# The low half of every strip of weights moved 128 bytes along its slot

## The chip, the core and the metric

One core of a Trainium2 chip runs the whole program. The metric is the device time of one execution in microseconds (us).

## What is computed

Three layers over 256 tokens of width 1024, batch 1, all in float32: a retention layer (four heads), a layer of latent attention (16 heads, causal), each with a gated side input, and a block with a 31-tap convolution, a multi-window pooling branch, an output mix and a gated feed-forward network of hidden width 2816. Nearly all of the time goes into products of an activation matrix with a weight matrix:

```python
for i in range(DEPTH):
    h = rms_norm(x, pre_norm_g[i])
    y = retention_branch(h, ...) if i % 2 == 0 else mla_branch(h, ...)
    x = x + rms_norm(y, post_norm_g[i])
    x = x + (p[i] @ ple_w_proj[i]) * jax.nn.sigmoid(x @ ple_w_gate[i])
# second block
proj = h @ w_in;  ...  mix = merged @ w_out
up = causal_dwconv(h @ w_up, w_dw_f, b_dw_f)
v, gt = jnp.split(up, 2, axis=-1)
f = (jax.nn.gelu(gt) * v) @ w_down
```

## The kernel before

The kernel reaches float32 accuracy with the faster float32r products: each operand is split into a high part (rounded to float32r) and a low part (the rest), and each product is made of three: high by high, high by low, low by high.

The weights are cut into 264 blocks of 128 partitions by 1024 elements (768 for the query blocks of the attention layer). SyncE loads a block from HBM into one of four slots of `raw`. ScalarE copies it, rounded, into the slot of the same number in `whi` (L990, in `split`); VectorE subtracts this from `raw` and writes the rest into `wlo` (L1521). TensorE takes the block from there. Both engines split three blocks ahead of TensorE (`AHEAD = 3`). A slot of `whi` or `wlo` is 1024 + 64 elements long (`SLOT_PAD`), so 4352 bytes, which is 17 times 256; the two tensors follow `raw` (4 slots of 4096 bytes) in the memory of each partition.

There are two kinds of block. In a **strip** the weights are the stationary operand: `products` (L486 to L502) takes eight tiles of 128 by 128, and for each issues three matmuls with 256 moving columns, one for each token: `whi` against the high part of the activations (L498), `whi` against their low part (L499), `wlo` against their high part (L500). Each matmul carries a weight load of its own (128 columns), which runs beside the matmul in front of it. In a **row block** the weights are the moving operand, 512 columns at a time, against a stationary tile of activations (`row_products`, L563 to L568, and two loops written out at L703 to L705 and L792 to L794). `row_block(b)` says which kind block b is.

Where a block lies in its slot hangs on the kind. `parts_of(b)` (L300), which both splits call, gives offset 0 for a row block and `STRIP_AT` = 16 elements, 64 bytes, for a strip, the same in `whi` and `wlo`; `products` reads with the same offset. Tiles, activations and slots all begin at multiples of 256 bytes counted from the start of `raw`, so the place of an operand within 256 bytes is 0 for all activations and all row blocks, and 64 for the strips. There is one exception: the first five blocks of the last product (`w_down`, blocks 242 to 246) are used as row blocks, but are split by the code of the loop in front of it, and so count as strips in `row_block`: they are moving operands that begin at 64.

The order of the work is fixed by semaphores (`lo_done` lets TensorE start a block, `pe_done` frees a slot for ScalarE). Some blocks are used unsplit from `raw` as plain float32 and are not touched by the change.

Of the kernel before, what the change touches and what calls it, by code (L numbers as in the profile page):

```python
# [28 lines left out]
P = 128  # L29
# [1 line left out]
D = 1024  # L31
DT = D // P
RING = 4
SLOT_PAD, STRIP_AT = 64, 16
AHEAD = 3
RET_HEADS, RET_V = 4, 512
MLA_HEADS, MLA_NOPE, MLA_ROPE = 16, 128, 64
# [50 lines left out]
def row_block(b):  # L88

    if b < B_RO:  # L90
        return b % 12 in range(4, 8)
    if B_GRP <= b < B_MO:
        return (b - B_GRP) % 12 == 1
    return b < B_MIN + 8 or B_MO <= b < B_WA or B_WO <= b < B_UP or b >= B_DN + 5
# [40 lines left out]
def program(nc, x_in, pre_in, p_in, pos_in, cols_in, rows_in, mask_in, tri_in, cnt_in, ident_in, ada_in, c_row, g_rows, w, out):  # L135

    ctx = ExitStack()
    with ctx:
        def sb(name, shape, dt=F32):
            return ctx.enter_context(nc.sbuf_tensor(name, shape, dt))  # L140
# [6 lines left out]
        whi = sb("whi", [P, RING, 1024 + SLOT_PAD], F32R)  # L147
        wlo = sb("wlo", [P, RING, 1024 + SLOT_PAD], F32R)
# [151 lines left out]
        def parts_of(b, n=1024):  # L300

            if b in KEPT:
                k = KEPT.index(b)
                a = Y[:, 4 * k:4 * k + 4, :, :].rearrange("p k c t -> p (k c t)")
                return a[:, 0:n], a[:, 1024:1024 + n]
            o = 0 if row_block(b) else STRIP_AT
            return whi[:, b % RING, o:o + n], wlo[:, b % RING, o:o + n]

        def used_first(b):

# [175 lines left out]
        def _(pe):  # L486
            mm = nc.tensor.matmul

            def products(base, parts, per=0, i=0, before=(), done=1):


                s = base % RING
                pe.wait_ge(lo_done, base + RING + 1 + per * i)
                for n, (t, a, o, start, stop) in enumerate(parts):
                    if n < len(before) and before[n]:
                        pe.wait_ge(*before[n])
                    c = slice(STRIP_AT + t * P, STRIP_AT + t * P + P)
                    mm(o, whi[:, s, c], a[:, 0, :], start=start, stop=False)  # L498
                    mm(o, whi[:, s, c], a[:, 1, :], start=False, stop=False)  # L499
                    last = mm(o, wlo[:, s, c], a[:, 0, :], start=False, stop=stop)  # L500
                if done:
                    last.then_inc(pe_done, 1)  # L502

# [33 lines left out]
            def strip(base, o, a, per=0, i=0, before=()):  # L537

                products(base, [(k, a[:, k, :, :], o, k == 0, k == 7) for k in range(8)], per, i, before)

            def free_a(k, per=0, i=0):

                pe.wait_ge(act_free, k + 1 + per * i)
                return GA[k % 2]

            def free_d(k, per=0, i=0):

                pe.wait_ge(dve_free, k + 1 + per * i)
                return GD[k % 2]
# [11 lines left out]
            def row_products(base, o, t, a, k0, start, stop, ks=(0, 1)):  # L561

                hi, lo = parts_of(base)  # L563
                for k in ks:
                    c = slice(512 * k, 512 * k + 512)
                    mm(o, a[:, k0 + k, 0, tok(t)], hi[:, c], start=start and k == 0, stop=False)  # L566
                    mm(o, a[:, k0 + k, 0, tok(t)], lo[:, c], start=False, stop=False)  # L567
                    last = mm(o, a[:, k0 + k, 1, tok(t)], hi[:, c], start=False, stop=stop and k == 1)  # L568
                return last
# [110 lines left out]
            b = free_d(V_HEAD + 1)  # L680
# [90 lines left out]
            def group(o, i, gates):  # L771
# [7 lines left out]
                for h in range(4):  # L779
                    out_k = GA[h // 2][:, T * (h % 2):T * (h % 2) + T]  # L780
                    parts += [(2 * h + k, S[:, 2 + k, :, :], out_k, k == 0, k == 1) for k in range(2)]
                pe.wait_ge(act_free, at(A_GRP + 1, 6))
                products(base, parts, 12, i, [None] * 4 + [(act_free, at(A_GRP + 2, 6))])

                pe.wait_ge(mo_gated, at(1, 4))
# [11 lines left out]
                def latent_strip(j, b):  # L797
                    products(base + j, [(k, Y[:, 16 + k, :, :], b, k == 0, k == 5) for k in range(6)],
                             12, i)
# [114 lines left out]
            for j in range(3, 8):  # L914
                if j % 2 == 0:
                    b = free_d(V_WA + j // 2)
                else:
                    b = GD[j // 2 % 2]
                strip(B_WA + j, halves(b)[j % 2], H, before=h_waits(U_LNA) if j == 3 else ())
            for j in range(4):  # L920
                if j % 2 == 0:
                    b = free_a(A_WP + j // 2)
# [4 lines left out]
            with pe.Fori(0, 2) as i:  # L927
                for j in range(4):
                    if j % 2 == 0:
                        b = free_a(A_WG + j // 2, 2, i)  # L930
                    plain_tokens(B_WG + j, halves(b)[j % 2], 4, i)
            for j in range(8, 16):
                if j % 2 == 0:
                    b = free_a(A_WG + j // 2)
# [9 lines left out]
            for j in range(4):  # L944
# [4 lines left out]
                b = bank[j]  # L949
# [25 lines left out]
        def _(act):  # L975
            activation = nc.scalar.activation

            def split(base, n=1024, per=0, i=0):

                b = base + AHEAD  # L980
                if b >= B_END:
                    return
                s = b % RING
                if b in SPARE:
                    act.wait_ge(spare_loaded[SPARE[b]], spare_count(b))
                else:
                    act.wait_ge(raw_loaded[s], raw_count(b) + 16 * (per // RING) * i)
                if b not in KEPT:
                    act.wait_ge(pe_done, used_first(b) + per * i)
                activation(parts_of(b + (per * i if isinstance(i, int) else 0), n)[0], block_in(b, n), ACT.Copy).then_inc(hi_done, 1)  # L990
# [518 lines left out]
        def _(dve):  # L1509
# [4 lines left out]
            def split(base, n=1024, per=0, i=0):  # L1514

                b = base + AHEAD
                if b >= B_END:
                    return
                hi, lo = parts_of(b + (per * i if isinstance(i, int) else 0), n)
                dve.wait_ge(hi_done, b + 1 + per * i)  # L1520
                tt(lo, block_in(b, n), f32(hi), ALU.subtract).then_inc(lo_done, 1)  # L1521
# [948 lines left out]
```

## Time and profile before

| | us |
|---|---|
| median of 3 runs | 828.81 (828.03 to 829.47) |
| the profiled execution, its own time | 828.66 |
| its span, first to last instruction | 826.9 |
| TensorE busy | 811.2 (98%) |
| VectorE busy | 661.9 (80%) |
| ScalarE busy | 456.8 (55%) |

The page counts a matmul as busy from its start to its modelled end, which lies beyond the start of the next one; busy time near 100% says that TensorE always had work, not how fast it took it. The rate shows in the distance from one start to the next. PE is TensorE's matmul stream, PEld its stream of weight loads, DVE VectorE, ACT ScalarE.

### The profile page before, as it was taken

How to read it: one execution, taken by the hardware profiler on the slowest of the kernel's cores; microseconds unless marked ns; L12 is line 12 of the kernel's file. 1: busy time of each engine (PE TensorE's matmuls, PEld its weight loads, DVE VectorE, ACT ScalarE, POOL GpSimd, SP SyncE). 2: the span in 40 equal slices, each digit the busy share in tenths (PEclk: the TensorE clock that was granted, in tenths of full speed). 3: DMA queues.
4: the chain of work that ended last, by engine and by line, in shares of the span. 5: the costliest groups of instructions: out<-in, count | busy, mean ns of one | idle time of the engine just before them, and what ended most of it. 6: DMA issues, size and time to landing. Idle time of an engine off the chain costs nothing.

```text
span 826.9 us, 14985 instructions
## 1 busy us (share of the span) xinstructions
PE 811.2 (98%) x5394; PEld 738.3 (89%) x5394; DVE 661.9 (80%) x1043; ACT 456.8 (55%) x682; POOL 43.4 (5%) x58
## 2 busy tenths in 40 slices
PE   9999999999999999999999999999999999999995
PEld 9898999988778999999988789988988999999884
DVE  5979887786966887787868778999898888888566
ACT  6464545565646665657565636115744777776440
POOL 0009000000011000000000000060000000000000
PEclk9999999999999999999999999999999999999998
DMA  6957675679735747383749572446571665565641
GB/s 223 363 201 265 209 260 190 238 253 361 256 139 166 261 147 268 119 285 111 271 170 335 183 254 106 136 150 212 187 248 58 229 202 182 192 209 207 201 154 51
DMA packets 49002, 170.57 MB, mean 206 GB/s; under 512 B 6080, under 2 KB 6720, under 8 KB 48960
## 3 DMA queue, kind: packets, MB, share of 16 engines
q1 hardware_dynamic: 40896, 143.23, 50.5%
q10 hardware_dynamic: 8064, 26.78, 9.3%
q8 instruction: 26, 0.43, 0.2%
q14 instruction: 16, 0.13, 0.1%
HBM read 168.93 MB, written 1.06 MB: 206 GB/s over the span
## 4 chain that ended last, share of the span: by engine, by line
PE 77%; DVE 13%; ACT 4%; issue 4%; DMA 1%; DVEq 1%; ACTq 0%
PE bank L498 12%; PE bank L500 12%; PE bank L499 12%; PE bank L566 8%; PE bank L568 8%; PE bank L567 8%; DVE bank L2011 4%; DVE wlo L1521 3%; PE bank L512 2%; PE bank L703 2%; PE bank L704 2%; PE bank L705 2%; DVE ada_raw L1533 1%; PE bank L609 1%; PE bank L852 1%
## 5 line engine op out<-in xcount | busy, mean ns | idle before, releaser
L990 ACT ACTIVATE whi<-raw 128x1024 fp32r<-128x1024 f32 (+1 forms) x236 | 244.2, 1041 | 198.3 <-PE bank L500 85.3
L1521 DVE TENSOR_TENSOR wlo<-raw,whi 128x1024 fp32r<-128x1024 f32 (+1 forms) x236 | 282.9, 1211 | 66.3 <-ACT whi L990 64.2
L498 PE MATMUL bank<-H,whi 128*128 128x256 f32 x816 | 230.8, 283 | 0.6 <-DVE wlo L1521 0.4
L499 PE MATMUL bank<-H,whi 128*128 128x256 f32 x816 | 227.7, 279 | 0.0
L500 PE MATMUL bank<-H,wlo 128*128 128x256 f32 x816 | 227.7, 279 | 0.0
L498 PEld LDWEIGHTS bank<-H,whi 128*128 128x128 f32 x816 | 153.8, 189 | 2.1 <-issue 1.2
L499 PEld LDWEIGHTS bank<-H,whi 128*128 128x128 f32 x816 | 154.7, 190 | 0.1
L500 PEld LDWEIGHTS bank<-H,wlo 128*128 128x128 f32 x816 | 153.2, 188 | 0.0
L566 PE MATMUL bank<-whi,Y 128*128 128x512 f32 x216 | 84.9, 393 | 0.3 <-DVE wlo L1521 0.3
L568 PE MATMUL bank<-whi,Y 128*128 128x512 f32 x216 | 84.3, 390 | 0.0
L567 PE MATMUL bank<-wlo,Y 128*128 128x512 f32 x216 | 84.2, 390 | 0.0
L1533 DVE CUSTOM_DVE_ANT_0 ada_raw<-ada_raw,crow 128x1024 f32<-128x1024 f32 x48 | 60.5, 1260 | 6.7 <-DMA ada_raw<-ada_in 6.3
L498 PE MATMUL bank<-Y,whi 128*128 128x256 f32 x176 | 50.1, 284 | 0.4 <-ACT G L1148 0.4
L499 PE MATMUL bank<-Y,whi 128*128 128x256 f32 x176 | 49.2, 280 | 0.0
L500 PE MATMUL bank<-Y,wlo 128*128 128x256 f32 x176 | 49.2, 279 | 0.0
L566 PEld LDWEIGHTS bank<-whi,Y 128*128 128x128 f32 x216 | 40.6, 188 | 9.0 <-DVE wlo L1521 0.7
L568 PEld LDWEIGHTS bank<-whi,Y 128*128 128x128 f32 x216 | 40.6, 188 | 8.7
L567 PEld LDWEIGHTS bank<-wlo,Y 128*128 128x128 f32 x216 | 40.6, 188 | 8.4
L2011 DVE SCALAR_TENSOR_TENSOR bank<-WK,cols,bank 128x256 f32<-128x256 f32 x116 | 47.4, 483 | 0.4
L566 PE MATMUL bank<-whi,H 128*128 128x512 f32 x112 | 44.3, 395 | 0.4 <-DVE H L1592 0.3
L567 PE MATMUL bank<-wlo,H 128*128 128x512 f32 x112 | 43.6, 390 | 0.0
L568 PE MATMUL bank<-whi,H 128*128 128x512 f32 x112 | 43.6, 389 | 0.0
(265 smaller groups left out, 1315.2 us busy)
## 6 DMA issues: line engine op xcount, KB each, us to landing
ada_raw<-ada_in ACTq DMA_DIRECT2D x48, 512.0 KB, 5.2
raw<-w_head SPq DMA_DIRECT2D x47, 512.0 KB, 4.5
raw<-w_up SPq DMA_DIRECT2D x42, 512.0 KB, 3.5
raw<-w_down SPq DMA_DIRECT2D x22, 512.0 KB, 3.4
raw<-w_uq SPq DMA_DIRECT2D x24, 384.0 KB, 3.1
raw<-w_ret_out SPq DMA_DIRECT2D x16, 512.0 KB, 5.1
raw<-w_mla_gate SPq DMA_DIRECT2D x16, 512.0 KB, 4.6
raw<-w_mla_out SPq DMA_DIRECT2D x16, 512.0 KB, 5.3
```

The source lines that it names most:

```text
L498: mm(o, whi[:, s, c], a[:, 0, :], start=start, stop=False)
L499: mm(o, whi[:, s, c], a[:, 1, :], start=False, stop=False)
L500: last = mm(o, wlo[:, s, c], a[:, 0, :], start=False, stop=stop)
L512: last = mm(o[:, tok(t)], raw[:, s, c], WT[:, t, c], start=(k == 0), stop=(k == 7))
L566: mm(o, a[:, k0 + k, 0, tok(t)], hi[:, c], start=start and k == 0, stop=False)
L567: mm(o, a[:, k0 + k, 0, tok(t)], lo[:, c], start=False, stop=False)
L568: last = mm(o, a[:, k0 + k, 1, tok(t)], hi[:, c], start=False, stop=stop and k == 1)
L703: mm(o, Hh[:, kk, tt], whi[:, s, c], start=(kk == 0), stop=False)
L990: activation(parts_of(b + (per * i if isinstance(i, int) else 0), n)[0], block_in(b, n), ACT.Copy).then_inc(hi_done, 1)
L1521: tt(lo, block_in(b, n), f32(hi), ALU.subtract).then_inc(lo_done, 1)
L1533: nc.vector.tensor_tensor_reduce(ada_raw[:, n, :], ada_raw[:, n, :], crow[:], 1.0, 0.0, ALU.mult, ALU.add, macc[:, a:a + 1]).then_inc(ada_ ...
L2011: stt(total[:, c, :], x, w_tap, CT[:, c, :], ALU.mult, ALU.add).then_inc(conv_tap[c], 1)
```

## The change

The one offset for strips becomes two: the high part stays at element 16 (64 bytes), the low part goes to element 48 (192 bytes). Row blocks stay at 0 in both. The slots keep their length: 48 + 1024 elements fit into 1088. No instruction is added, removed or put in another place; the offsets of what VectorE writes at L1521 and of what TensorE reads at L500 change, and, for blocks 242 to 246, of what it reads as the low moving operand at L567.

```diff
-SLOT_PAD, STRIP_AT = 64, 16
+SLOT_PAD, ROW_AT, STRIP_HI, STRIP_LO = 64, 0, 16, 48
...
-            o = 0 if row_block(b) else STRIP_AT
-            return whi[:, b % RING, o:o + n], wlo[:, b % RING, o:o + n]
+            h, l = (ROW_AT, ROW_AT) if row_block(b) else (STRIP_HI, STRIP_LO)
+            return whi[:, b % RING, h:h + n], wlo[:, b % RING, l:l + n]
...
-                    c = slice(STRIP_AT + t * P, STRIP_AT + t * P + P)
-                    mm(o, whi[:, s, c], a[:, 0, :], start=start, stop=False)
-                    mm(o, whi[:, s, c], a[:, 1, :], start=False, stop=False)
-                    last = mm(o, wlo[:, s, c], a[:, 0, :], start=False, stop=stop)
+                    hi = whi[:, s, STRIP_HI + t * P:STRIP_HI + t * P + P]
+                    lo = wlo[:, s, STRIP_LO + t * P:STRIP_LO + t * P + P]
+                    mm(o, hi, a[:, 0, :], start=start, stop=False)
+                    mm(o, hi, a[:, 1, :], start=False, stop=False)
+                    last = mm(o, lo, a[:, 0, :], start=False, stop=stop)
```

## Rows read from the trace of the kernel before

**Rows 1.** The page: busy time by engine, then the chain that ended last.

```profile
PE 811.2 (98%) x5394; PEld 738.3 (89%) x5394; DVE 661.9 (80%) x1043; ACT 456.8 (55%) x682; POOL 43.4 (5%) x58
PE 77%; DVE 13%; ACT 4%; issue 4%; DMA 1%; DVEq 1%; ACTq 0%
```

**Rows 2.** Groups by line, shapes apart, whole span: count, busy us, mean ns, idle before.

```profile
L498 PE MATMUL bank<-H,whi 128*128 128x256 f32 x816 | 230.8, 283 | 0.6 <-DVE wlo L1521 0.4
L498 PE MATMUL bank<-Y,whi 128*128 128x256 f32 x176 | 50.1, 284 | 0.4 <-ACT G L1148 0.4
L498 PE MATMUL bank<-S,whi 128*128 128x256 f32 x40 | 11.5, 287 | 0.7 <-ACT G L1287 0.7
```

**Rows 3.** Timeline of PE, strips of `w_conv_in` and `w_pool_in`: start, length, instruction.

```profile
509.52 0.28 PE L500 MATMUL bank<-H,wlo 128*128 128x256 f32 x1
...
528.22 0.28 PE L500 MATMUL bank<-H,wlo 128*128 128x256 f32 x1
```

**Rows 4.** Timeline of PE, the forty strips of `w_up` (third and last matmul).

```profile
645.18 0.28 PE L500 MATMUL bank<-H,wlo 128*128 128x256 f32 x1
...
757.89 0.28 PE L500 MATMUL bank<-H,wlo 128*128 128x256 f32 x1
```

**Rows 5.** Timeline of PE, slow trains: head gates, attention latents, `w_pool` with `w_pw`.

```profile
50.63 0.28 PE L499 MATMUL bank<-H,whi 128*128 128x256 f32 x1
...
61.70 0.28 PE L500 MATMUL bank<-H,wlo 128*128 128x256 f32 x1
...
278.69 0.28 PE L498 MATMUL bank<-Y,whi 128*128 128x256 f32 x1
...
289.17 0.28 PE L500 MATMUL bank<-Y,wlo 128*128 128x256 f32 x1
...
579.45 0.28 PE L499 MATMUL bank<-H,whi 128*128 128x256 f32 x1
...
590.52 0.28 PE L500 MATMUL bank<-S,wlo 128*128 128x256 f32 x1
```

**Rows 6.** Timeline of PE, `w_down`: blocks 242 to 246, then aligned row blocks.

```profile
758.25 0.40 PE L567 MATMUL bank<-wlo,Y 128*128 128x512 f32 x1
...
772.01 0.40 PE L566 MATMUL bank<-whi,Y 128*128 128x512 f32 x1
...
775.22 0.39 PE L568 MATMUL bank<-whi,Y 128*128 128x512 f32 x1
...
814.89 0.39 PE L566 MATMUL bank<-whi,Y 128*128 128x512 f32 x1
```

**Rows 7.** Groups by line, PEld, 510 to 528 us.

```profile
L498 PEld LDWEIGHTS bank<-H,whi 128*128 128x128 f32 x54 | 10.1, 188 | 0.0
L499 PEld LDWEIGHTS bank<-H,whi 128*128 128x128 f32 x53 | 9.9, 188 | 0.0
L500 PEld LDWEIGHTS bank<-H,wlo 128*128 128x128 f32 x53 | 9.9, 188 | 0.0
```

**Rows 8.** The same, 660 to 740 us.

```profile
L499 PEld LDWEIGHTS bank<-H,whi 128*128 128x128 f32 x227 | 43.6, 192 | 0.0
L498 PEld LDWEIGHTS bank<-H,whi 128*128 128x128 f32 x227 | 42.6, 188 | 0.0
L500 PEld LDWEIGHTS bank<-H,wlo 128*128 128x128 f32 x227 | 42.6, 188 | 0.0
```

**Rows 9.** The splits by line: DVE 660 to 740 and 775 to 815 us, ACT in the latter.

```profile
L1521 DVE TENSOR_TENSOR wlo<-raw,whi 128x1024 fp32r<-128x1024 f32 x30 | 36.6, 1220 | 8.8 <-ACT whi L990 8.8
...
L1521 DVE TENSOR_TENSOR wlo<-raw,whi 128x1024 fp32r<-128x1024 f32 x13 | 15.9, 1226 | 15.4 <-ACT whi L990 15.3
...
L990 ACT ACTIVATE whi<-raw 128x1024 fp32r<-128x1024 f32 x13 | 13.8, 1060 | 20.1 <-PE bank L568 19.9
```

**Rows 10.** Windows: us, then PE, PEld, DVE, ACT, POOL busy (count), granted clock, DMA share, GB/s.

```profile
510.00:528.00 18.00, 18.00 (x162) 18.00 (x160) 17.61 (x35) 5.42 (x9) 0.00 (x0) 1.00 0.55 195
660.00:740.00 80.00, 80.00 (x682) 80.00 (x681) 66.85 (x104) 57.75 (x86) 0.00 (x0) 1.00 0.59 193
759.00:771.00 12.00, 12.00 (x53) 9.74 (x52) 8.21 (x11) 7.07 (x10) 0.00 (x0) 1.00 0.59 189
```

## The prediction

> **What bounds the kernel now.** First the page. TensorE is busy 811.2 of 826.9 us, and the chain that ended last runs through it for 77% [rows 1]. So the time is the number of matmuls times the distance from one start to the next. Then the groups by line: L498 ran 816 + 176 + 40 = 1032 times, and L499 and L500 as often, so strips hold 3096 matmuls of 256 columns; their idle time in front is under 1 us a group [rows 2]. The change touches the operand of 1032 of them.
>
> Then the timeline, for the distance, and here is what the busy shares hide. In the strips of `w_conv_in` and `w_pool_in` 165 steps take 528.22 - 509.52 = 18.70 us, 113.3 ns each [rows 3]. In the strips of `w_up` 957 steps take 757.89 - 645.18 = 112.71 us, 117.8 ns each [rows 4]. It is the same code, slots, tiles of H and offsets, and the granted clock is 1.00 in both [rows 10]. A strip train thus runs in one of two steady rhythms, 4.44 ns apart. The slow one holds in `w_up` (958 matmuls), in three trains like 50.63 to 61.70 us (94 steps in 11.07 us, 117.8 ns), four like 278.69 to 289.17 (89 or 90 steps, 117.8 ns) and one from 579.45 to 590.52 (94 steps) [rows 4, 5]: 958 + 3 x 95 + 4 x 91 + 95 = 1702 matmuls. The other 1394 run at or near 113.3.
>
> The weight loads show what differs. In the fast rhythm the three loads of a triple last 188 ns each [rows 7]; in the slow one the load of L499 lasts 192 and the other two 188 [rows 8], although L498 and L499 load the same tile from the same bytes. So the slow rhythm repeats every three matmuls: 3 x 117.8 = 353.3 ns against 3 x 113.3 = 340.0, which is 13.3 ns more, two steps of 6.67.
>
> That 6.67 ns stands by itself in the last product. Blocks 242 to 246 are moving operands that begin at byte 64 against stationary tiles at 0: 59 steps take 772.01 - 758.25 = 13.76 us, 233.2 ns each. Behind them the moving operand begins at 0 and 175 steps take 39.67 us, 226.7 ns each [rows 6]. A matmul whose two operands stand 64 bytes apart the wrong way costs 6.6 ns more, with all else equal. From this I read that the stream of the moving operand and the load of the next stationary one get in each other's way when both reach the same part of a repeating range of bytes. The range is at most 256 bytes: slots are 17 x 256 bytes apart, and no slot runs differently from the others within `w_up`.
>
> **The change part by part.** *The split on VectorE.* L1521 takes 1220 ns where it writes at 64 and 1226 where it writes at 0 [rows 9]. The output offset is worth 6 ns at most; at 192 I take nothing. Bounds: -6 to +6 ns by the 140 blocks split as strips, under 1 us of VectorE work, and hidden. In `w_up`, where the cover is thinnest, one strip takes 24 x 117.8 = 2.83 us; VectorE is busy 66.85 us in 80, so 2.36 us per strip, ScalarE 57.75, so 2.04 [rows 10]. If TensorE goes to its fast rhythm, a strip takes 24 x 113.3 = 2.72 us and both still fit, so the gain isn't handed to another engine. The DMA moves 193 GB/s there and would need 201. ScalarE's L990 writes where it wrote.
>
> *Blocks 242 to 246.* They hold 60 matmuls, 20 of them with the low part moving. If these 20 lose their 6.6 ns, -0.13 us; if all 60 do, -0.4; if each of the 20 pays it twice, +0.13. I take nothing.
>
> *The low weight load of a strip.* This is the change. No trace of before shows a strip with its low tile at 192, so bounds from the nearest rows. On the good side every slow train goes to the fast rhythm: 1702 x 4.44 ns = 7.6 us less. On the bad side the low load sits 64 bytes on the other side of the moving operand within 256 bytes, the relation of blocks 242 to 246, and each costs 6.67 ns: in the 1394 fast matmuls 465 x 6.67 = 3.1 us more; in all, 1032 x 6.67 = 6.9 us more. If instead the fast trains fall into the slow rhythm, 1394 x 4.44 = 6.2 us more.
>
> Which is likelier? The slow rhythm is one in which three identical loads fall into unequal places, the next triple repeating them. It lives on each load being like the one before. With one load in three displaced by 128 bytes the pattern can't stay as it is in 1702 matmuls, and it is the larger stock: 7.6 us can be won against 6.2 lost. Whether it resolves to 340 ns or to 346.7 (one step of 6.67 left) can't be read off; the latter gives 1702 / 3 x 6.67 = 3.8 us less. I take 3.8, which is also half of the way.
>
> The Trainium skill speaks against any effect. "TensorE: Matmul & The Clock Gate", Part 2, step by step, states that the array has two independent read ports into SBUF, and that loading the next weights takes no bandwidth from the running matmul. "SBUF — State Buffer", Specifications (TRN2), gives 16-byte cachelines, and 64 and 192 are both multiples of 16. By these the sum would be 0. The trace disagrees for a moving operand: 64 bytes cost 6.6 ns [rows 6]. For a stationary one no row decides.
>
> *The sum.* 828.66 (the profiled execution: span 826.9 and 1.8 around it) - 3.8 = 824.9. The median of the runs is 0.15 higher, so 825.0.
>
> **The rivals.**
>
> *Same.* The range that repeats is 128 bytes, not 256. Then 64 and 192 are the same place and nothing changes: 828.8. For it: nothing in the trace tells 128 from 256; slots and tiles begin at multiples of both. Also here: gains and losses cancel, say half of the slow trains won (-3.8) and 3.1 us lost in the fast ones, -0.7. By the skill's rule of separate ports the time would be this one too; the rows bear that rule out for nothing here except the equal length of the splits. Against it: the two rhythms are only 4% apart and start from small differences, so to leave 3096 matmuls untouched asks for exact equality. 0.27.
>
> *Slower.* One mechanism: the low load, now 64 bytes behind the moving operand in place of 64 ahead, meets it, and the matmul beside it waits 6.67 ns. For it: blocks 242 to 246 are that relation and pay it in each of 59 steps [rows 6]. Against it: there the moving operand is 512 columns long and the load takes under half of it. It decides from the point at which more matmuls pay than are freed: 465 in the fast trains alone give +3.1 us, 831.9; if the slow trains keep theirs and all low loads pay, 828.8 + 6.9 = 835.7. The nearer value is 831.9, since in the slow trains two steps per triple are paid already. 0.28.
>
> *The change doesn't do what it says*: not here. Both splits go through `parts_of`, and `products` reads with the same constants.
>
> **How the numbers follow.** Forecast (faster): 0.45 at 825.0, from 821.2 (all slow trains fast) to 827. Same: 0.27. Slower: 0.28, at 831.9. The range must reach from the full gain to most of the slower case: 828.8 - 7.6 - 0.4 = 820.8, and 832.5 above, which leaves out some 0.03 below and 0.12 above (fast trains fallen to the slow rhythm: 835.0; or all low loads paying). The forecast's own range is 821 to 827. A measurement here tells about 0.2%, 1.7 us, from no change. Of the faster case some 0.03 lies within that, and of the slower as much: faster 0.43, same 0.32, slower 0.25.
>
> **What the changed kernel's profile would show.** The distance of starts in `w_up`: 113.3 if the slow rhythm is gone, 115.6 if one step is left, 117.8 if nothing changed, over 118 if the low load pays on top. The distance in the strips of `w_conv_in`: 113.3 if the fast rhythm is untouched, 115.6 if the low load pays, 117.8 if it fell. The weight loads of L498, L499 and L500: if L500 alone now lasts longer, the displaced load is the one that waits. Blocks 242 to 246: whether L567 has a distance of its own. L1521 should stay at 1220 ns, and the idle time in front of L498 under 1 us; if it grows, the cover by VectorE was too thin. The prediction is wrong if the strips' rhythms stand as they were, or if the fast trains are the ones that changed.

## The result: 822.34 us, and every train of strips in the fast rhythm

| | before | changed |
|---|---|---|
| median | 828.26 (824.41 to 829.47, 9 runs) | 822.34 (821.67 to 823.03, 9 runs) |
| ratio, 95% interval | | 0.993 (0.9916 to 0.9944) |
| profiled execution, its span | 828.66, 826.9 | 821.67, 819.6 |

The changed kernel is 0.7% faster. The page, engines first and then the chain, answers to [rows 1]; the instructions are the same in number:

```profile
PE 803.2 (98%) x5394; PEld 729.8 (89%) x5394; DVE 660.8 (81%) x1043; ACT 457.1 (56%) x682; POOL 43.4 (5%) x58
```

```profile
PE 74%; DVE 15%; ACT 4%; issue 4%; DMA 2%; DVEq 1%; ACTq 0%
```

8 us went from TensorE's busy time, and 7.3 us from the span. The timeline of PE of the changed kernel (start, length, instruction; lines are one higher than before) answers to [rows 3], [rows 4], [rows 5] for the first head and [rows 6] for blocks 242 to 246, in that order:

```profile
506.36 0.28 PE L501 MATMUL bank<-H,wlo 128*128 128x256 f32 x1
...
525.08 0.28 PE L501 MATMUL bank<-H,wlo 128*128 128x256 f32 x1
...
642.14 0.28 PE L501 MATMUL bank<-H,wlo 128*128 128x256 f32 x1
...
750.81 0.28 PE L501 MATMUL bank<-H,wlo 128*128 128x256 f32 x1
...
49.59 0.28 PE L500 MATMUL bank<-H,whi 128*128 128x256 f32 x1
...
60.25 0.28 PE L501 MATMUL bank<-H,wlo 128*128 128x256 f32 x1
...
751.15 0.40 PE L568 MATMUL bank<-wlo,Y 128*128 128x512 f32 x1
...
764.74 0.39 PE L567 MATMUL bank<-whi,Y 128*128 128x512 f32 x1
```

The strips of `w_conv_in` and `w_pool_in`, fast before, take 18.72 us for 165 steps: as they were. Those of `w_up` take 108.67 us for 957 steps, 113.6 ns each, where they took 112.71. The head's train takes 10.66 for 94 steps where it took 11.07. Blocks 242 to 246 take 13.59 us for 59 steps, 230.3 ns each, where they took 13.76. (A train is a run of strip matmuls without a wait between them; a step is the distance from one start to the next.)

The fast rhythm isn't there from the first matmul. By the starts in the trace, 22 of the 27 trains of over 30 matmuls begin with some distances of 116 to 124 ns, a dozen at most, and then settle at 113.3; `w_up` has six such distances. Summed over these trains, what lies above 113.33 ns a step is 0.7 us, where before it was 7.7. The weight loads of the changed kernel, 660 to 740 us, answer to [rows 8]:

```profile
L501 PEld LDWEIGHTS bank<-H,wlo 128*128 128x128 f32 x236 | 44.3, 188 | 0.0
L499 PEld LDWEIGHTS bank<-H,whi 128*128 128x128 f32 x236 | 44.3, 188 | 0.0
L500 PEld LDWEIGHTS bank<-H,whi 128*128 128x128 f32 x235 | 44.1, 188 | 0.0
```

None in this window lasts 192 any more, and 236 triples fit where there were 227. The split and the window that holds it answer to [rows 9, 10]:

```profile
L1522 DVE TENSOR_TENSOR wlo<-raw,whi 128x1024 fp32r<-128x1024 f32 x31 | 37.9, 1222 | 6.4 <-ACT whi L991 6.4
```

The window of 660 to 740 us (span, then busy time and count of PE, PEld, DVE, ACT and POOL, clock, DMA share, GB/s):

```profile
660.00:740.00 80.00, 80.00 (x708) 80.00 (x707) 69.19 (x106) 61.01 (x90) 0.00 (x0) 1.00 0.60 208
```

VectorE's split costs what it did (1222 ns against 1220), and its share rose to 86%, but it hands nothing on to TensorE.

One new wait did appear. In the timeline of the changed kernel, at the fifth strip of `w_up`, ScalarE's row in a fence of its own and the rows of PE behind it:

```profile
652.07 0.60 ACT L1477 ACTIVATE WK<-bank 128x512 f32<-128x512 f32 x1
```

```profile
652.70 0.28 PE L501 MATMUL bank<-H,wlo 128*128 128x256 f32 x1
652.91 0.36 PE L499 MATMUL bank<-H,whi 128*128 128x256 f32 x1
653.10 0.28 PE L500 MATMUL bank<-H,whi 128*128 128x256 f32 x1
653.22 0.28 PE L501 MATMUL bank<-H,wlo 128*128 128x256 f32 x1
```

The fifth strip writes the bank of the first again and has to wait until ScalarE has copied it out (L1477, which ends at 652.67). The profile doesn't name this wait, but seven of the fourteen traces of this study have a pause at this matmul, of 200 to 406 ns from start to start, and in each the next matmul starts 0.24 or 0.29 us after the end of that copy. TensorE arrives there 0.4 us earlier than in the slow rhythm and loses 0.2 us with the restart behind it.

### The profile page after: what moved, and what is told of

It is laid out like the page before. It is cut to its first block, busy times and chain, and to the rows that moved or that the text cites. A ratio compares the mean times of both kernels' runs of the same rounds, so it can differ in the third digit from the quotient of the medians.

```text
span 819.6 us, 14985 instructions
## 1 busy us (share of the span) xinstructions
PE 803.2 (98%) x5394; PEld 729.8 (89%) x5394; DVE 660.8 (81%) x1043; ACT 457.1 (56%) x682; POOL 43.4 (5%) x58
## 4 chain that ended last, share of the span: by engine, by line
PE 74%; DVE 15%; ACT 4%; issue 4%; DMA 2%; DVEq 1%; ACTq 0%
PE bank L499 11%; PE bank L501 11%; PE bank L500 11%; PE bank L567 9%; PE bank L569 8%; PE bank L568 8%; DVE bank L2012 4%; DVE wlo L1522 3%; PE bank L513 2%; PE bank L704 2%; PE bank L705 2%; DMA ada_raw<-ada_in 2%; PE bank L706 2%; DVE ada_raw L1534 1%; PE bank L610 1%
## 5 line engine op out<-in xcount | busy, mean ns | idle before, releaser
L500 PE MATMUL bank<-H,whi 128*128 128x256 f32 x816 | 225.6, 277 | 0.0
L500 PEld LDWEIGHTS bank<-H,whi 128*128 128x128 f32 x816 | 153.4, 188 | 0.1
L567 PE MATMUL bank<-whi,Y 128*128 128x512 f32 x216 | 84.7, 392 | 0.3 <-DVE wlo L1522 0.3
L567 PEld LDWEIGHTS bank<-whi,Y 128*128 128x128 f32 x216 | 40.6, 188 | 9.2 <-DVE wlo L1522 0.9
L500 PE MATMUL bank<-Y,whi 128*128 128x256 f32 x176 | 48.6, 276 | 0.0
L567 PE MATMUL bank<-whi,H 128*128 128x512 f32 x112 | 44.3, 395 | 0.4 <-DVE H L1593 0.3
```

Source lines behind the costliest of these rows:

```text
L500: mm(o, hi, a[:, 1, :], start=False, stop=False)
```

## The experiments

Offsets below are those of the high and low part of a strip in bytes; before is 64 and 64, the change 64 and 192. Each run differs from the changed kernel only in the lines shown (`hold1`: from the kernel before), and the whole computation is done. The runs were made in three series on three chips, each with executions of the kernel before beside it; a ratio compares within its series.

Since each execution of some of these kernels can come out in one of two groups of times, the median alone misleads; the ranges are given, and the rhythm comes from the trace of one execution.

### Is it the distance between the parts, or the place?

Theory A of the expectations says that the difference between the two parts counts, theory B that 192 is a better place than 64. Both at 192:

```diff
-SLOT_PAD, ROW_AT, STRIP_HI, STRIP_LO = 64, 0, 16, 48
+SLOT_PAD, ROW_AT, STRIP_HI, STRIP_LO = 64, 0, 48, 48
```

> Both parts of a strip at byte 192 of the slot (after: high 64, low 192; before: both 64). Theory A, the difference: the slow rhythm (117.8 ns per strip matmul, repeating every three) needs three weight loads at the same place, and the changed kernel is fast because one of three stands apart. It expects the slow rhythm back in w_up (117.8 ns from start to start) and the time near before, 826 to 829 us. Theory B, the place: 192 is a better place than 64 against a moving operand that begins at 0. It expects 113.3 ns in w_up and 821 to 823 us, or better, since now all three loads are there.

Measured: 828.4 us (825.14 to 831.83), ratio to before 1.0012 (0.9987 to 1.0038). In the trace most of `w_up` runs at 117.8 ns, other trains at 113.4 or 117.8, and not the same ones as before: the strips of `w_conv_in` are slow here. So 192 as such is no better place than 64, and theory B is out. The groups by line of this kernel, PEld, 665 to 745 us, which lie in the slow part of `w_up`:

```profile
L501 PEld LDWEIGHTS bank<-H,wlo 128*128 128x128 f32 x227 | 42.7, 188 | 0.0
L499 PEld LDWEIGHTS bank<-H,whi 128*128 128x128 f32 x227 | 42.6, 188 | 0.0
L500 PEld LDWEIGHTS bank<-H,whi 128*128 128x128 f32 x227 | 42.4, 187 | 0.0
```

It is the slow rhythm of before [rows 4], and no load lasts 192. So a load of 192 ns, as in [rows 8], doesn't mark the slow rhythm; only the distance of starts does.

The roles exchanged:

```diff
+SLOT_PAD, ROW_AT, STRIP_HI, STRIP_LO = 64, 0, 48, 16
```

> High part at 192, low part at 64: the same distance of 128 bytes with the roles exchanged. Theory A (the difference counts) expects all strip trains at 113.3 ns and 821 to 823 us. Theory B (192 is the better place) expects two thirds of the loads in the good place, so 113.3 ns too or a rhythm between; no more than 825 us. A third theory, C, that it is the low part's load beside the long-waiting second matmul that has to be at 192, expects 117.8 ns in w_up and 828 us.

Measured: 828.48 us (824.04 to 829.97), ratio 1.0009 (0.9983 to 1.0036). Two rhythms again, 113.3 ns and a slow one of 118.9. In the traced execution, one of the lower group (825.64 us), `w_up` is fast, and slow are among others trains like this one of a head (timeline of PE):

```profile
82.17 0.28 PE L500 MATMUL bank<-H,whi 128*128 128x256 f32 x1
...
87.64 0.28 PE L501 MATMUL bank<-H,wlo 128*128 128x256 f32 x1
```

46 steps in 5.47 us are 118.9 ns. A distance of 128 bytes is thus not enough. Theory A falls in its plain form, and C, which put all of `w_up` at 117.8, doesn't fit the trace either. Of the places tried, only the high part at 64 with the low part at 192 leaves one fast rhythm.

The low part 64 bytes from the high one:

```diff
+SLOT_PAD, ROW_AT, STRIP_HI, STRIP_LO = 64, 0, 16, 32
```

> High part at 64, low part at 128: 64 bytes apart in place of 128. Theory A in its wide form (any difference within 256 bytes breaks the slow rhythm) expects 113.3 ns in w_up and 821 to 823 us. In its narrow form (half of the range apart) it expects the slow rhythm or one between, 115 to 118 ns and 825 to 829 us.

Measured: 831.94 us (831.61 to 832.57), ratio 1.0073 (1.0044 to 1.0102), one group of times, and one rhythm in all trains of the trace. The timeline of PE of this kernel, third and last matmul of `w_up`:

```profile
647.78 0.28 PE L501 MATMUL bank<-H,wlo 128*128 128x256 f32 x1
...
760.91 0.27 PE L501 MATMUL bank<-H,wlo 128*128 128x256 f32 x1
```

957 steps in 113.13 us are 118.2 ns. The narrow form of A comes nearest, though it had 829 us as its upper end, and it doesn't fit `swapped`.

The low part at 160:

```diff
+SLOT_PAD, ROW_AT, STRIP_HI, STRIP_LO = 64, 0, 16, 40
```

> High part at 64, low part at 160, between 128 (118.2 ns in all strip trains) and 192 (113.3 in all). If places count in steps of 64 bytes with a shift of a whole step needed, the low load at 160 still waits in part: 114 to 118 ns, 824 to 831 us. If what counts is only that the low part is beyond 128, 113.3 ns and 822 us.

Measured: 831.66 us (831.19 to 832.18), ratio 1.0068 (1.0038 to 1.0099); 117.8 ns in every train. So 32 bytes short of 192 the slow rhythm is not only possible but the only one in the trace. Beyond 192 no place within the same 256 bytes was tried.

The low part at 0:

```diff
+SLOT_PAD, ROW_AT, STRIP_HI, STRIP_LO = 64, 0, 16, 0
```

> High part at 64, low part at 0: 64 bytes apart on the other side than in the run with the low part at 128, which had one rhythm, 118.2 ns. If the sign doesn't matter, 118.2 ns again and 832 us. If the low part has to stay clear of one place only, 113.3 ns in all trains and 822 us, or two rhythms as before.

Measured: 833.16 us (831.26 to 836.17), ratio 1.007 (1.0046 to 1.0095); 117.8 ns nearly everywhere, and 122.3 in one train (566.47 to 575.03 us, 70 steps in 8.56 us). Seven of the ten executions took 831.3 to 833.5 us and three 836.0 to 836.2, so there are two groups here too; what parts them wasn't looked into. The sign of the distance is of little weight: both neighbours of 64 make all trains slow.

### How long is the range that repeats?

The low part 256 bytes on, with slots one 256-byte step longer:

```diff
+SLOT_PAD, ROW_AT, STRIP_HI, STRIP_LO = 128, 0, 16, 80
```

> High part at 64, low part at 320, slots 128 elements longer than a block in place of 64, so still at multiples of 256 bytes: within 256 bytes both parts stand where they stood in the kernel before, but 256 bytes apart. If the place counts within 256 bytes only (my reading), the rhythms are those of before: 117.8 ns in w_up, 826 to 829 us. If any distance between the parts does it, or the range is 512 bytes, 113.3 ns and 821 to 823 us.

Measured: 828.46 us (824.55 to 831.33), ratio 1.002 (0.9994 to 1.0046), and the two rhythms of before. The timeline of PE of this kernel shows both, in a head's train and in the strips of `w_conv_in`:

```profile
88.18 0.28 PE L500 MATMUL bank<-H,whi 128*128 128x256 f32 x1
...
98.50 0.28 PE L501 MATMUL bank<-H,wlo 128*128 128x256 f32 x1
...
508.92 0.28 PE L501 MATMUL bank<-H,wlo 128*128 128x256 f32 x1
...
528.35 0.28 PE L501 MATMUL bank<-H,wlo 128*128 128x256 f32 x1
```

91 steps in 10.32 us are 113.4 ns, 165 in 19.43 are 117.8. In the trace of before it was the other way round for these two [rows 3, 5]. For the strips 256 bytes more thus change nothing that the trace or the times show.

For blocks 242 to 246, whose moving operands lie at 64 (high) and 320 (low) here, they do. The timeline of PE of this kernel:

```profile
757.65 0.39 PE L568 MATMUL bank<-wlo,Y 128*128 128x512 f32 x1
...
771.17 0.39 PE L567 MATMUL bank<-whi,Y 128*128 128x512 f32 x1
```

59 steps in 13.52 us are 229.2 ns, where the kernel before, with both parts at 64, took 233.2 [rows 6]. So a range of 256 bytes holds for the strips as far as they show it, and not for these moving operands. The longer slots move the start of each slot too, so whether 256 bytes or the new places of the slots do it stays open.

Both at 128:

```diff
+SLOT_PAD, ROW_AT, STRIP_HI, STRIP_LO = 64, 0, 32, 32
```

> Both parts of a strip at 128. So far: both at 0 gives 120.0 ns in every train and all three weight loads at 192 ns (each matmul pays 6.67 ns over 113.3); both at 64 or both at 192 give 113.3 or 117.8. If places repeat every 128 bytes for equal parts, 128 is like 0: 120.0 ns, 835 to 837 us. If they repeat every 256 bytes only, 128 is farthest from the moving operand's 0 and should be clear of it: 113.3 ns and 822 us, or two rhythms.

Measured: 834.6 us (834.46 to 835.43), ratio 1.0107 (1.0071 to 1.0144); 118.7 ns in `w_up` (958 steps in 113.67 us) and most trains, 120.0 in others. Nearly as bad as 0, but not the same, so neither expectation is met, and the place farthest from the moving operand's 0 isn't clear of it. With 64 and 192 in one slot working as no equal pair does, 128 bytes isn't the range: the changed kernel itself would be the kernel before.

### What does the worst place cost?

Both at 0, where the moving operand begins:

```diff
+SLOT_PAD, ROW_AT, STRIP_HI, STRIP_LO = 64, 0, 0, 0
```

> Both parts of a strip at 0, where the moving operand begins too. If only the distance between the parts mattered, this is the kernel before: two rhythms, 824 to 829.5 us. If the place against the moving operand counts, some other rhythm, and I expect a slower one, 118 to 120 ns in all trains, 3096 x 5 to 7 ns above the fast floor of 822: 837 to 843 us at worst. Blocks 242 to 246 begin at 0 here and should run at 226.7 ns from the first.

Measured: 835.9 us (835.08 to 836.76), ratio 1.0108 (1.0065 to 1.015). The groups by line of this kernel, PEld 665 to 745 us, and then its timeline of PE for `w_up`:

```profile
L499 PEld LDWEIGHTS bank<-H,whi 128*128 128x128 f32 x223 | 42.8, 192 | 0.0
L500 PEld LDWEIGHTS bank<-H,whi 128*128 128x128 f32 x223 | 42.8, 192 | 0.0
L501 PEld LDWEIGHTS bank<-H,wlo 128*128 128x128 f32 x222 | 42.6, 192 | 0.0
```

```profile
650.11 0.28 PE L501 MATMUL bank<-H,wlo 128*128 128x256 f32 x1
...
764.94 0.28 PE L501 MATMUL bank<-H,wlo 128*128 128x256 f32 x1
```

957 steps in 114.83 us are 120.0 ns. This is the clean case: each matmul pays 120.0 - 113.3 = 6.7 ns, the figure that blocks 242 to 246 gave [rows 6]. The time is a little under the 837 to 843 us that I had expected at worst, and blocks 242 to 246, at 0 here, run at 227.0 ns.

Whole numbers of this step, spread over a repeating pattern, give the other rhythms too. The slow one of before is two steps in three matmuls (353.3 ns against 340.0). The 118.7 of `both128` is four in five (593.3 against 566.7), the 118.9 of `swapped` five in six (713.3 against 680), the 122.3 of `low0` four in three (366.7), the 118.2 of `low128` eleven in fifteen (1773.3 against 1700). The sums of so many successive distances in these trains keep to these values within 2 ns. A step isn't one matmul that pays 6.67 ns while its neighbour pays nothing, however. In the timeline of PE of before, slow rhythm of `w_up`, each of the three distances is 0.11 to 0.12 us:

```profile
645.30 0.28 PE L498 MATMUL bank<-H,whi 128*128 128x256 f32 x1
645.41 0.28 PE L499 MATMUL bank<-H,whi 128*128 128x256 f32 x1
645.53 0.28 PE L500 MATMUL bank<-H,wlo 128*128 128x256 f32 x1
645.65 0.28 PE L498 MATMUL bank<-H,whi 128*128 128x256 f32 x1
```

In `low160` the same sum of 353.3 ns falls on them as 123, 116 and 114.

The moving side, with the low part of the row blocks at 192 and their high part at 0:

```diff
-            h, l = (ROW_AT, ROW_AT) if row_block(b) else (STRIP_HI, STRIP_LO)
+            h, l = (ROW_AT, STRIP_LO) if row_block(b) else (STRIP_HI, STRIP_LO)
...
-                            mm(o, Hh[:, kk, tt], wlo[:, s, c], start=False, stop=False)
+                            mm(o, Hh[:, kk, tt], wlo[:, s, STRIP_LO + 512 * k:STRIP_LO + 512 * k + 512], start=False, stop=False)
```

(and the same at the other loop written out.)

> The changed kernel, with the low part of row blocks at 192 too (high part stays at 0), so that the low moving operand of 512 columns begins at 192 against a stationary tile at 0. In the changed kernel blocks 242 to 246 (high 64, low 192) run at 230.4 ns for each matmul, other row blocks at 226.7. If the low one alone pays 6.67 ns, row blocks run at 228.9 ns: 1130 matmuls by 2.2 ns, 2.5 us more, 824 to 826 us. If it costs nothing without the high part's 64, 822 us. The strips should not change.

Measured: 824.22 us (823.4 to 825.37), ratio to before 0.9988 (0.9968 to 1.0007); 1.9 us over the changed kernel, and 2.3 over `aligned_down` below, of the same series. Its timeline of PE in the row blocks of `w_mla_out`:

```profile
440.06 0.39 PE L568 MATMUL bank<-wlo,Y 128*128 128x512 f32 x1
...
459.97 0.39 PE L568 MATMUL bank<-wlo,Y 128*128 128x512 f32 x1
```

87 steps in 19.91 us are 228.9 ns, as expected: 6.67 ns in three matmuls. The strips stayed at 113.3. So a moving operand of 512 columns at 192 against a stationary tile at 0 pays, while a stationary tile at 192 against a moving operand of 256 columns at 0, in the changed kernel, doesn't.

### One part of the change alone

```diff
-            h, l = (ROW_AT, ROW_AT) if row_block(b) else (STRIP_HI, STRIP_LO)
+            h, l = (ROW_AT, ROW_AT) if row_block(b) else (STRIP_HI, STRIP_LO if b >= B_UP else STRIP_HI)
...
-                    lo = wlo[:, s, STRIP_LO + t * P:STRIP_LO + t * P + P]
+                    low_at = STRIP_LO if base >= B_UP else STRIP_HI
+                    lo = wlo[:, s, low_at + t * P:low_at + t * P + P]
```

> The low part at 192 only in the strips of w_up (and blocks 242 to 246), at 64 in all others: one part of the change alone. So far equal parts (64 and 64, 192 and 192) show two rhythms, 113.3 and 117.8 ns, and executions in two groups 4.3 us apart; 64 with 192 shows one. The theory (each train falls into a rhythm as it starts; the displaced low load leaves only the fast one) expects w_up at 113.3 ns in every execution, the other trains as in the kernel before, and one group of times at 823.5 to 826 us. The rival, that the offsets act over the whole program, expects two groups again.

Measured: 824.42 us (823.83 to 825.48, ten executions), ratio 0.997 (0.995 to 0.999), one group. The kernel before, on the same chip, fell into 8 executions at 823.69 to 825.29 and 17 at 827.86 to 829.9. The timeline of PE: `w_up` first, a train of latents behind it.

```profile
645.37 0.28 PE L502 MATMUL bank<-H,wlo 128*128 128x256 f32 x1
...
754.04 0.28 PE L502 MATMUL bank<-H,wlo 128*128 128x256 f32 x1
...
278.37 0.28 PE L500 MATMUL bank<-Y,whi 128*128 128x256 f32 x1
...
288.86 0.28 PE L502 MATMUL bank<-Y,wlo 128*128 128x256 f32 x1
```

`w_up` takes 108.67 us for 957 steps, the same as in the changed kernel; the latents take 10.49 for 89, 117.9 ns, as before [rows 5]. The part made its own train fast, and it took away the upper group of times. Which other trains are slow isn't fixed even for the same code: a train of 71 matmuls from 563.23 us is slow here (117.8 ns) and was fast in the trace of before, and the one at 579.63 is fast and was slow [rows 5]. Both run before `w_up`, and nothing in them was changed. The two groups of the kernel before lie as far apart as `w_up` in one rhythm and in the other (958 x 4.44 = 4.3 us), so this train's rhythm is the likely cause of the two groups. No execution of the kernel before in its lower group was traced, so that rests on this run and on the traces of its relatives: `swapped`, traced in its lower group, has `w_up` fast, and `hold1` below, `both192` and `low320`, traced in their upper groups, have it slow.

### What chooses the rhythm?

The offsets of before, one plain matmul more in front of the strips of `w_up`:

```diff
+            hold(GD[0], 1)
             strips_a(B_UP + 4, A_UP + 2, 10, U_LNB)
```

> The offsets of the kernel before, with one more plain float32 matmul of 128 columns (0.11 us) put in front of the strips of w_up. The theory that a train's rhythm is chosen as it starts expects this to move the choice: w_up at 113.3 ns in all or most executions (one group at 824 to 825.5 us), or at 117.8 in all (828 to 829.5). If the rhythm is chosen by something outside TensorE's own stream (the splits or the DMA), the two groups stay in about the shares of before, 10 of 26 in the lower one.

Measured: 827.9 us (824.34 to 829.5), ratio 1.0002 (0.998 to 1.0024), 2 of 10 executions in the lower group against 8 of 25 for before. That doesn't settle it: the shares can't be told apart. The strips of `w_conv_in`, which run before the added matmul, are slow in this trace (510.20 to 529.75 us, 117.8 ns) and were fast before [rows 3]. And the trace caught a change of rhythm. The timeline of PE of this kernel:

```profile
645.95 0.28 PE L500 MATMUL bank<-H,wlo 128*128 128x256 f32 x1
...
656.51 0.28 PE L500 MATMUL bank<-H,wlo 128*128 128x256 f32 x1
656.72 0.35 PE L498 MATMUL bank<-H,whi 128*128 128x256 f32 x1
656.92 0.28 PE L499 MATMUL bank<-H,whi 128*128 128x256 f32 x1
...
758.44 0.28 PE L500 MATMUL bank<-H,wlo 128*128 128x256 f32 x1
```

The first 93 steps take 10.56 us, 113.5 ns; then comes the wait of the fifth strip, 0.1 us; behind it 862 recorded steps take 101.52 us, 117.8 ns. With both parts at 192 the same wait (245 ns from start to start) did the same. In the changed kernel, in the one with `w_up` alone displaced and in `swapped` it was followed by the fast rhythm.

Within a train the two directions differ. In none of the 371 trains of over 30 matmuls in the fourteen traces does the fast rhythm give way to the slow one; that happened only over a wait. The other way it is common: a train begins with slow distances and settles at 113.3 ns within a dozen matmuls, in 22 of 27 trains of the changed kernel and in 11 of 26 of the kernel before, where it took four at most. So the slow rhythm comes in with a restart of the stream, and the offsets decide whether it lasts: with 64 and 192 it never did. What decides between the two where both can last isn't shown.

### A version with the last product aligned

Blocks 242 to 246 at 0, for which the last two passes of the loop of `w_up` on ScalarE and VectorE are written out:

```diff
-    return b < B_MIN + 8 or B_MO <= b < B_WA or B_WO <= b < B_UP or b >= B_DN + 5
+    return b < B_MIN + 8 or B_MO <= b < B_WA or B_WO <= b < B_UP or b >= B_DN
...
-            with act.Fori(0, 10) as i:
+            with act.Fori(0, 8) as i:
                 up_pass(1, i)
+            up_pass(9, 0)
+            up_pass(10, 0)
```

> The changed kernel with blocks 242 to 246 at 0 like the other row blocks (the last two passes of the loop of w_up on ScalarE and VectorE are written out for that). These 60 matmuls should go from 230.4 to 226.7 ns: 0.22 us less, 821.5 to 822.5 us, not told apart from the changed kernel by its time, but by the distance of starts.

Measured: 821.95 us (821.35 to 822.98, ten executions), ratio to before 0.9954 (0.9935 to 0.9974), where the executions of before in that series had a median of 824.49, with 13 of 21 in the lower group. The blocks run at 226.7 ns (timeline of PE, the same two matmuls as above):

```profile
751.29 0.40 PE L568 MATMUL bank<-wlo,Y 128*128 128x512 f32 x1
...
764.69 0.39 PE L567 MATMUL bank<-whi,Y 128*128 128x512 f32 x1
```

13.40 us for 59 steps are 227.1 ns with the first few behind the strips, against 13.59: 0.2 us less, as worked out. The time can't tell it from the changed kernel.

## Why the prediction was right, point by point

**What bounds the kernel.** Right. The whole gain is in the distance of starts in strips. Adding up all distances under 190 ns between a strip's matmul and the next gives 354.0 us before and 346.6 after, 7.4 less, for a span 7.3 shorter (two distances fewer are counted after, 0.2 us, so it is nearer 7.1 for equal counts).

**The size of the gain.** The direction was right and the size at half: I took 3.8 us, and 7.0 came in the profiled execution (828.66 to 821.67). The step that was mis-sized is the resolution of the slow rhythm: I left open 340 or 346.7 ns per triple and took the latter. It went to 340.0 in every train, and the upper bound of the sum, 1702 x 4.44 = 7.6 us, was nearly the value. Taken from it are the slow first matmuls of most trains, which leave 0.7 us above the fast rhythm where the trains that were fast before had little, and the wait and restart at the fifth strip of `w_up`, 0.2 us; blocks 242 to 246 add 0.17. I had said that both splits still fit in 2.72 us per strip, which held; the evacuation of the bank behind the first strips I hadn't looked at.

**The median.** It fell by 5.9, not 7.0, because the kernel before has two groups of times and its median lies among them. I took the range of its three shown runs, 828.03 to 829.47, for the whole spread; the three later series held 10 of 26, 8 of 25 and 13 of 21 executions in the lower group, from 823.3 us on. A trace with two rhythms for the same code should have made me expect that.

**The reason.** Half right. That the slow rhythm repeats every three matmuls and holds two steps of 6.67 ns is borne out: `both0` shows the step alone (120.0 ns), and the other rhythms are whole numbers of it. That the load of 192 ns shows where the slow rhythm waits is not: one load of three lasts 192 where two steps are paid, in `both0` all three, and in the slow rhythms of `both192` and `low160` none. Nor is it that the slow rhythm lives on the three loads being alike: with 64 and 128, 64 and 160 and 192 and 64 the loads are unlike, and slow rhythms of 118.2, 117.8 and 118.9 ns exist. So a displaced load as such doesn't break the pattern, and I had the right outcome partly by luck of the place chosen; three of the four other ways to set the low part apart from a high part at 64 in this study (128, 160, 0) made it slower, and the fourth (320) changed nothing.

**The rivals.** *Same*, by a range of 128 bytes: out, by the change itself. That the range is at most 256 bytes, which I had read from slots that all run alike, is right for the strips as far as `low320` shows it and wrong for the moving operands of blocks 242 to 246, 229.2 ns with the low part 256 bytes on against 233.2. By the Trainium skill's rule of two independent read ports ("TensorE: Matmul & The Clock Gate", Part 2, step by step) offsets would cost nothing; the runs disagree, with 835.9 against 822.3 us for 0 and 0 against 64 and 192, the work being equal. That it is the two reads which meet is not shown: no run moves the activations, so a place that is bad against the other operand and one that is bad by itself can't be told apart. *Slower*, because the low load at 192 would stand to the moving operand as in blocks 242 to 246: this took a moving operand displaced for the same thing as a stationary one displaced the other way. `row_low192` shows the moving one paying at 192, the changed kernel's strips show the stationary one not paying. A low part in the wrong place does cost time (at 128, 0 or 160: 3 to 5 us more than before), but the place was another.

**The small terms.** L1521 costs the same at 192 (1222 ns): right. Blocks 242 to 246: bounded at -0.4 to +0.13, measured 13.59 against 13.76 us, -0.17.

## What to carry to other kernels

Where TensorE is always busy, read the distance from one start to the next, for equal matmuls in several places of the trace: two values for the same code are a stall that no busy share shows, and may be why executions fall into groups. Where the high and the low part of the weights begin within a slot is worth a sweep of a few offsets: here 13.6 us lie between best and worst at no cost in instructions. Judge such a sweep by the trace and by ten executions, not by three.

## What the runs showed of the hardware

The distance of starts of float32r matmuls of 256 columns with a weight load each, moving operand at 0, granted clock 1.00, by the places of the high and low tile:

| high, low | ns | median us |
|---|---|---|
| 64, 192 | 113.3, slower in the first dozen at most | 822.3 |
| 64, 64 (also 64, 320; 192, 192) | 113.3 or 117.8 | 828.2 to 828.5, spread over 5 to 7 us |
| 192, 64 | 113.3 or 118.9 | 828.5, two groups |
| 64, 160 | 117.8 | 831.7 |
| 64, 128 | 118.2 | 831.9 |
| 64, 0 | 117.8, one train 122.3 | 833.2, two groups |
| 128, 128 | 118.7 to 120.0 | 834.6 |
| 0, 0 | 120.0 | 835.9 |

The series of executions differ by chip, so medians 1 us apart shouldn't be ranked. The median of 64 and 64 was 828.2 to 828.5 in three series and 824.5 in the fourth, where the lower group held more executions.

With 512 columns and the stationary tile at 0: moving at 0 and 0 226.7 ns, 0 and 192 228.9, 64 and 320 229.2, 64 and 192 230.3, 64 and 64 233.2, 192 and 192 233.3. Stationary and moving operand both at 0 are thus the best place with 512 columns and the worst with 256. The step in the rhythms worked out above is 6.67 ns, 16 cycles at 2.4 GHz.

Why the places cost what they do is open. That two readers of the same 64 bytes of every 256 stand in each other's way is near at hand and isn't shown. Against it are the pair at 128, nearly as slow as the pair at 0 where the moving operand begins; the low part at 160, as bad as at 128; and the blocks with their low part at 320. The splits write to the places that TensorE reads, and no run keeps the two apart; but the distances keep their pattern within 2 ns whether VectorE is writing or not, which speaks against the writes. The slow rhythm held for up to 959 matmuls without a break.
